# First shift and scale in four batches, k-outer projections, and a later place for the slabs that VectorE weighs

## What is computed

```python
mod = jax.nn.silu(c) @ w_ada[l] + b_ada[l]
shift1, scale1, gate1, shift2, scale2, gate2 = jnp.split(mod[:, None, :], 6, axis=-1)
h = rms_norm(x, g_norm1[l]) * (1.0 + scale1) + shift1
proj = h @ w_in[l]
na_q, na_k, na_v, q_lat, kv_lat, k_rot, gate_na, gate_mla = jnp.split(proj, split_at, axis=-1)
qa = rms_norm(na_q.reshape(B, S, NA_HEADS, NA_HEAD_DIM), g_na_q[l])
ka = rms_norm(na_k.reshape(B, S, NA_HEADS, NA_HEAD_DIM), g_na_k[l])
```

## Time and profile before

| | us |
|---|---|
| three runs | 1152.79, 1153.98, 1155.91 |
| median | 1153.98 |
| the profiled execution's own time | 1156.07 |
| its span | 1154.20 |
| TensorE matmul busy | 1102.4 (96%) |
| VectorE busy | 408.7 (35%) |
| ScalarE busy | 298.5 (26%) |
| mean granted TensorE clock | 0.982 of full |

### The profile page before, as it was taken

One profiled execution on the slowest core, in us unless ns is written; L12 is line 12 of the kernel. 1 busy time (PEld: TensorE's weight loads), 2 busy tenths in 40 slices (PEclk: granted clock), 3 DMA queues, 4 the chain that ended last, 5 costly groups with the idle time before them and its releaser, 6 DMA issues.

```text
span 1154.2 us, 18227 instructions
## 1 busy us (share of the span) xinstructions
PE 1102.4 (96%) x7154; PEld 740.6 (64%) x7154; DVE 408.7 (35%) x993; ACT 298.5 (26%) x635; POOL 53.4 (5%) x85
## 2 busy tenths in 40 slices
PE   5899999999999899998899999999899999999998
PEld 2787686688756445544555455554368888887567
DVE  0599765532724121221212122212134111341951
ACT  1214324601511121221211112112123121212951
POOL 0010202003000000000000000000001001100001
PEclk8899899999999999998999999999999999999999
DMA  9999447944699999999999999999994334230000
GB/s 384 384 403 411 164 146 299 420 194 183 263 367 412 408 410 377 410 410 364 410 380 410 397 410 409 395 410 409 411 372 145 111 114 157 79 125 1 1 1 37
DMA packets 75495, 334.51 MB, mean 290 GB/s; under 512 B 8432, under 2 KB 9808, under 8 KB 59792
## 3 DMA queue, kind: packets, MB, share of 16 engines
q1 hardware_dynamic: 73008, 327.97, 72.2%
q10 hardware_dynamic: 2176, 3.37, 0.8%
q0 software_dynamic: 224, 1.97, 0.4%
HBM read 332.23 MB, written 1.05 MB: 289 GB/s over the span
## 4 chain that ended last, share of the span: by engine, by line
PE 83%; DMA 10%; DVE 4%; SPq 1%; issue 1%; ACT 1%; ACTq 0%; DVEq 0%
PE bank L930 13%; PE bank L490 11%; PE bank L974 7%; DMA ring<-experts 7%; PE bank L812 5%; PE bank L832 5%; PE bank L1065 5%; PE bank L886 4%; PE bank L1166 2%; PE bank L505 2%; PE bank L722 2%; PE bank L1117 2%; PE bank L737 2%; PE bank L397 2%; DMA ring<-stream 2%; PE bank L556 2%
## 5 line engine op out<-in xcount | busy, mean ns | idle before, releaser
L930 PE MATMUL bank<-ring,arena 128*32 128x512 f32 (+1 forms) x1120 | 182.0, 626 | 16.9 <-DMA ring<-experts 16.7
L490 PE MATMUL bank<-hT,ring 128*128 128x256 f32 x704 | 156.9, 384 | 1.7 <-ACT hT L1359 1.7
L490 PEld LDWEIGHTS bank<-hT,ring 128*128 128x128 f32 x704 | 134.9, 193 | 23.1 <-issue 4.6
L930 PEld LDWEIGHTS bank<-ring,arena 128*32 128x32 f32 (+1 forms) x1120 | 52.3, 124 | 127.7 <-issue 127.4
L974 PE MATMUL bank<-ring,arena 128*32 128x512 f32 (+1 forms) x560 | 87.5, 596 | 2.0 <-DMA ring<-experts 2.0
L812 PE MATMUL bank<-arena 128*128 128x128 bf16 x1152 | 72.2, 219 | 1.1 <-ACT arena L1516 1.1
L812 PEld LDWEIGHTS bank<-arena 128*128 128x128 bf16 x1152 | 66.9, 98 | 8.0 <-issue 5.0
L832 PE MATMUL bank<-arena 128*128 128x512 bf16 x288 | 66.1, 379 | 0.0
L2122 DVE TENSOR_TENSOR arena<-bank,arena 128x512 f32<-128x512 f32 x48 | 33.2, 692 | 92.3 <-ACT arena L1542 92.3
L2110 DVE SCALAR_TENSOR_TENSOR arena<-bank,arena 128x256 f32<-128x256 f32 x24 | 11.6, 484 | 145.2 <-ACT arena L1535 141.3
L1293 POOL TENSOR_TENSOR hT<-hT 128x256 f32<-128x256 f32 x30 | 21.8, 726 | 859.1 <-ACT hT L1353 857.7
(11 more groups left out here) (369 smaller groups left out, 1435.7 us busy)
## 6 DMA issues: line engine op xcount, KB each, us to landing
ring<-experts SPq DMA_DIRECT2D x384, 512.0 KB, 11.3
ring<-stream SPq DMA_DIRECT2D x118, 1024.0 KB, 9.3
arena<-consts POOLq DMA_DIRECT2D x1, 1664.0 KB, 11.7
resid<-x SPq DMA_DIRECT2D x1, 1024.0 KB, 5.3
resid<-ctx ACTq DMA_DIRECT2D x1, 1024.0 KB, 12.5
arena<-stream SPq DMA_DIRECT2D x1, 1024.0 KB, 9.3
arena<-rpb ACTq DMA_DIRECT2D x2, 438.0 KB, 25.7
out<-arena SPq DMA_DIRECT2D x3, 256.0 KB, 2.3
```

The source lines that it names most:

```text
L490: mm = mmul(o[:, 0:n_tok], w[:, k, t * P:(t + 1) * P], hT[:, k, 0:n_tok], start=(k == 0), stop=(k == KT - 1))
L930: mm = mmul(o[at:at + n_slots, :], xg[:, kk, at:at + n_slots], w[g][:, k, :], start=(kk == 0), stop=(kk == KT - 1))
```

## The change

ada1 0 to 7 become four batches ("first", i) of two slabs, i and i+4, so that each gives the shift and the scale of k = 2i and 2i+1; each batch has its own copy, fold, bias, gain, two scales and two shifts. The projections qk0 and qk1 run k-outer: after each batch, both tiles of a slab advance by two k (two_ks: four matmuls), each of their four tiles in a bank of its own (0 to 3); part of qk2 runs between (banks 4 and 5). The slab order begins ada1 0, 4, in0, ada1 1, 5, in1, ada1 2, 6, 3, 7, in2, in3. The sums over the heads' squares of all eight tiles move behind the tiles of qk3 and vna0, in banks 6 and 7. ScalarE issues its three loads of constants behind the fourth copy. The weighed slabs stand later in the stream: eight up to in7, then one each behind in7, gate stage 0, ukv and gate stage 1. VectorE weighs 0 to 7 before the latents' means, 8 and 9 behind the latents, 10 and 11 ahead of the drains of msum. TensorE adds the sums in gate stages 1, 2, 3, 5 and 6.

```diff
--- before.py
+++ after.py
@@ -338,13 +338,21 @@

         GATE_FILL = [[("ada1", 8)], [], [("ada1", 21)], [("ada1", 22)], [], [], [], [("ada1", 23)]]
         SIDE = list(range(9, 21))
+        SIDE_SUMS = {1: range(0, 4), 2: range(4, 6), 3: range(6, 8), 5: range(8, 10), 6: range(10, 12)}
         side_slabs = []
-        ADA_BATCHES = [("ada1", 0, 8), ("ada1", 8, 16), ("ada2", 0, 12), ("ada2", 12, 12)]
+        ADA_BATCHES = {1: ("ada1", 8, 16), 2: ("ada2", 0, 12), 3: ("ada2", 12, 12)}
+        FIRST_BATCHES = [("first", i) for i in range(4)]

         def ada_batch(which, j):
-            for n, (w, lo, count) in enumerate(ADA_BATCHES):
+
+            if which == "ada1" and j < 8:
+                return ("first", j % 4), j // 4
+            for n, (w, lo, count) in ADA_BATCHES.items():
                 if w == which and lo <= j < lo + count:
                     return n, j - lo
+
+        def batch_size(batch):
+            return 2 if batch in FIRST_BATCHES else ADA_BATCHES[batch][2]

         EARLY = [("na", i) for i in range(4)] + [("mla", i) for i in range(4)]
         FIRST_FILL = [("ada2", j) for j in range(4)]
@@ -387,7 +395,7 @@
                 w, n = take_slab((which, j))
                 w = w.rearrange("p (k c) -> p k c", k=8)
                 batch, r = ada_batch(which, j)
-                first, last = r == 0, r == ADA_BATCHES[batch][2] - 1
+                first, last = r == 0, r == batch_size(batch) - 1
                 if first:
                     open_group((batch, "quarters"), 6)
                 o = bk((batch, "quarters"))
@@ -606,26 +614,82 @@
             pe.wait_ge(S("ones_set"), 1)
             rms_sums("sum1", 0, 256, squared="sq1")
             pe.wait_ge(S("silu_c"), 1)
-            for j in range(8):
-                ada_slab("ada1", j)
+
+            in_at = {}
+
+            def first_inputs(slab, t, ks):
+
+                name = (f"qk{slab}", t)
+                if slab not in in_at:
+                    in_at[slab] = take_slab(("in", slab))[1]
+                o = open_group(name, 2 * slab + t) if ks[0] == 0 else bk(name)
+                for k in ks:
+                    h_tile("h1", k)
+                    mm = mmul(o[:, 0:256], eight(in_at[slab])[:, k, t * P:(t + 1) * P], hT[:, k, 0:256], start=(k == 0), stop=(k == KT - 1))
+                if ks[-1] == KT - 1:
+                    close_group(mm, name)
+                    if t == 1:
+                        slab_end[in_at[slab]] = name
+
+            def head_squares(j):
+                pe.wait_ge(S("sq_qk"), j + 1)
+                o = open_group(("qkn", j), 6 + j % 2)
+                close_group(mmul(o[:, 0:256], cc("bones"), sqt[:, j % 2, 0:256], start=True, stop=True), ("qkn", j))
+
+            def two_ks(slab, i):
+                for t in range(2):
+                    first_inputs(slab, t, (2 * i, 2 * i + 1))
+
+            ada_slab("ada1", 0)
+            ada_slab("ada1", 4)
             pe.wait_ge(S("fold_in"), 16)
-            ada_fold(0)
-
-            for s in range(4):
-                t_tiles(f"qk{s}", ("in", s), 2, [1, 2], 256, ready="h1" if s == 0 else None)
-                for i in ((0,), (1,), (2, 3), (4, 5))[s]:
-                    leave_to_vector(i)
-                for t in range(2):
-                    j = 2 * s + t
-                    pe.wait_ge(S("sq_qk"), j + 1)
-                    o = open_group(("qkn", j), 3 + j % 2)
-                    close_group(mmul(o[:, 0:256], cc("bones"), sqt[:, j % 2, 0:256], start=True, stop=True), ("qkn", j))
-            for s in range(2):
-                tok_tiles(f"vna{s}", ("in", 4 + s), 2, [1, 2])
-                for i in ((6, 7), (8, 9))[s]:
-                    leave_to_vector(i)
+            ada_fold(("first", 0))
+            two_ks(0, 0)
+            ada_slab("ada1", 1)
+            ada_slab("ada1", 5)
+            ada_fold(("first", 1))
+            two_ks(1, 0)
+            two_ks(0, 1)
+            two_ks(1, 1)
+            ada_slab("ada1", 2)
+            ada_slab("ada1", 6)
+            ada_fold(("first", 2))
+            ada_slab("ada1", 3)
+            two_ks(0, 2)
+            ada_slab("ada1", 7)
+            two_ks(1, 2)
+            ada_fold(("first", 3))
+            first_inputs(2, 0, range(0, 6))
+            two_ks(0, 3)
+            two_ks(1, 3)
+            first_inputs(2, 0, range(6, KT))
+            first_inputs(2, 1, range(KT))
+
+            w, n = take_slab(("in", 3))
+            w = w.rearrange("p (k c) -> p k c", k=8)
+            for i in (0, 1):
+                leave_to_vector(i)
+            for t in range(2):
+                o = open_group(("qk3", t), t)
+                for k in range(KT):
+                    mm = mmul(o[:, 0:256], w[:, k, t * P:(t + 1) * P], hT[:, k, 0:256], start=(k == 0), stop=(k == KT - 1))
+                close_group(mm, ("qk3", t))
+                head_squares(2 * t)
+                head_squares(2 * t + 1)
+            slab_end[n] = ("qk3", 1)
+            _, n = take_slab(("in", 4))
+            for i in (2, 3):
+                leave_to_vector(i)
+            for t in range(2):
+                tok_tile(("vna0", t), n, t, 2 + t)
+                head_squares(4 + 2 * t)
+                head_squares(5 + 2 * t)
+            slab_end[n] = ("vna0", 1)
+            tok_tiles("vna1", ("in", 5), 2, [1, 2])
+            for i in (4, 5):
+                leave_to_vector(i)
             t_tiles("ql", ("in", 6), 2, [1, 2], 256)
-            for i in (10, 11):
+            for i in (6, 7):
                 leave_to_vector(i)
             w, n = take_slab(("in", 7))
             w = w.rearrange("p (k c) -> p k c", k=8)
@@ -640,6 +704,7 @@
                               start=(kk == 0), stop=(kk == 1))
             close_group(mm, "krot4")
             slab_end[n] = "krot4"
+            leave_to_vector(8)
             pe.wait_ge(S("sq_ql"), 2)
             rms_sums("sum_ql", 5, 256, tiles=2, src=lambda k: sqt[:, k, 0:256])
             pe.wait_ge(S("sq_kvl"), 1)
@@ -652,12 +717,12 @@
                 t_tiles(f"gt{s}", ("in", 8 + s), 2, [1, 2], 256)
                 for f in GATE_FILL[s]:
                     ada_slab(*f)
-                if s < 2:
-                    for i in range(6 * s, 6 * s + 6):
-                        side_sum(i)
+                for i in SIDE_SUMS.get(s, ()):
+                    side_sum(i)

             pe.wait_ge(S("small_set"), 4)
             gate_tiles(0)
+            leave_to_vector(9)

             pe.wait_ge(S("qln"), 2)
             w, n = take_slab(("uq", 0))
@@ -682,7 +747,9 @@
                 o = open_group(("uv", t), 1 + t % 2)
                 close_group(mmul(o[:, :], lat[:, 2, t * P:(t + 1) * P], w[:, 512:1024], start=True, stop=True), ("uv", t))
             slab_end[n] = ("uv", 1)
+            leave_to_vector(10)
             gate_tiles(1)
+            leave_to_vector(11)

             gate_tiles(2)
             o = open_group("mq_sums", 3)
@@ -1334,8 +1401,9 @@
             def ada_quarters(batch):

                 full(act, (batch, "quarters"))
-                if batch:
-                    full(act, (batch - 1, "columns"))
+                before = dict(zip(FIRST_BATCHES[1:] + [1, 2, 3], FIRST_BATCHES + [1, 2])).get(batch)
+                if before:
+                    full(act, (before, "columns"))
                 emptied(a.copy(quarters[:], bk((batch, "quarters"))[:, 0:256]), (batch, "quarters"))

             def root(n, src, tag, cols, parts=P):
@@ -1344,10 +1412,6 @@
                 a.activation(src[0:parts, 0:cols], src[0:parts, 0:cols], ACT.Sqrt).then_inc(S(tag + "_rt"), 1)

             root(1, rstd, "n1", 256)
-            ada_quarters(0)
-            act.dma_start(cs[:, C_EARLY:C_W], consts_d[:, C_EARLY:C_W]).then_inc(S("const_in"), 16)
-            act.dma_start(stat[0:96, 0:256].bitcast(I32), pos_d).then_inc(S("const_in"), 16)
-            act.dma_start(ve[:, V_EARLY:V_W], vecs_d[:, V_EARLY:V_W]).then_inc(S("const_in"), 16)
             def square(tag, k, side=0):

                 a.activation(hT[:, k, T * side:T * side + T], xT[:, side, k, :], ACT.Square).then_inc(S(tag), 1)
@@ -1363,8 +1427,14 @@
                 a.activation(mark2[0:1, 0:1], ones[0:1, 0:1], f)


-            for k in range(KT):
-                shift("h1", k, mod1[:, k:k + 1])
+            for i in range(4):
+                ada_quarters(("first", i))
+                if i == 3:
+                    act.dma_start(cs[:, C_EARLY:C_W], consts_d[:, C_EARLY:C_W]).then_inc(S("const_in"), 16)
+                    act.dma_start(stat[0:96, 0:256].bitcast(I32), pos_d).then_inc(S("const_in"), 16)
+                    act.dma_start(ve[:, V_EARLY:V_W], vecs_d[:, V_EARLY:V_W]).then_inc(S("const_in"), 16)
+                for k in (2 * i, 2 * i + 1):
+                    shift("h1", k, mod1[:, k:k + 1])
             for r in range(2):
                 src = bass.AP(rpb_d.tensor, (5 - r) * 31 - 48, [[1, 64], [15 * 31, 8], [1, RUN]])
```

(36 more changed lines are left out.)

## The result

The changed kernel takes 1161.57 us in the median of five runs (1159.87 to 1163.94) against 1153.98 for the kernel before. The ratio, estimated from all runs, is 1.0054, with a 95% interval of 1.0028 to 1.0081: a small loss, but clear of no change. In a second batch it was 1160.40 against 1155.49, ratio 1.0060 (1.0039 to 1.0081). The forecast was 1152.6 with a range of 1148 to 1159: the sign is wrong and the median lies outside. The profiled execution took 1159.87 us with a span of 1158.1; before's had 1154.20.

What follows compares the result with a forecast made beforehand. VectorE's chain was taken as the new bound. Gate stage 3 2.55 us earlier, side sums +0.28 and an early clock spell +0.9 gave -1.4 from the median 1153.98: 1152.6 us, range 1148.0 to 1159.0.

Steps and rivals of the forecast that it cites:

- The hole in the loads: in3 waits for qk0 to close at 41.6; stream loses 8 us, taken as nothing; as rival up to 3 us, 14%.
- Front, TensorE: TensorE's start through qk3: first projection piece at 17.0, end at 47.7 us, from full-clock prices.
- clock spell at the front, 0.9: TensorE's idle from 14.2 to 17.0 may drop the clock for one piece: 0 to 1.7 us, 0.9 taken.
- loses 1: TensorE, ready at 59.8, waits for the bank of head squares 4 and 5, emptied at 60.6.
- 10.4 us like for like: Front's gain by the end of the third projected slab: 59.8-1.7-47.7.
- From the latent mean to the first shuffle 22.67: VectorE's old stretch, carried over; slabs 8 and 9 add 7.82, putting the shuffle at 116.3 us.
- The third sum at the end of weighing plus 0.4: Third sum of squares waits for slabs 10 and 11, weighed by 137.6, and starts at 138.0 us.
- Clock behind the wait, 2.6: Low clock after the wait for the drains, before gate stage 3: between 0 and 3.4 us, 2.6 taken.
- 36.90 plus 0.28 for four side sums: Gate stage 3 to the scores: 36.90 us as before, plus 0.28 for four side sums now there.
- The hole costing nothing: Rival, 17%: before the third sum of squares, clock holds or recovers (1150.0), or drains are not held (1143.4).
- The early clock staying low until 34 us: Slower rival, 17%: low clock from near 17 us shifts VectorE's chain by 6.5, total 1158.2 us.
- the 21% for slower: Whole kernel: chance of a time above 1157.5 us, 0.15 of it from the early clock staying low.

Runs made afterwards that it cites:

- late2: The changed kernel with the weighing of slabs 10 and 11 put behind VectorE's four drains of the sums of squares: 1156.72 us, ratio 1.0020.
- late4: The changed kernel with slabs 8 to 11 weighed behind the four drains, their places in the stream moved to match: 1150.71 us, ratio 0.9957.
- warm_hole: The changed kernel with five idle matmuls in TensorE's wait between second and third sum of squares: 1162.15 us, ratio 1.0039.
- sqrt_early: The changed kernel with ScalarE's table for roots loaded right behind the sines: 1161.13 us, ratio 1.0043.
- mix: late4 with side sums in two lots, gate stage 3 between one-column groups two and three, key square sums in banks 0 and 5: 1156.09 us, ratio 0.9994.
- mix2: As mix, but gate stage 3 in banks 0 and 5 and the sums of squares in 1 and 2 again: 1152.08 us, ratio 0.9972.

## Why the prediction was wrong

**The way the change works was right in its main steps.** The hole in the loads (no bytes at 36 to 38 us), TensorE's wait ahead of the one-column sums (3.12, "some 2.5" forecast), the wait for the drains between second and third sum (3.73, "some 5"), and the low clock behind it all came at the places named. late2 and late4 show that the weighing of slabs 8 to 11 makes both waits. The rule from the Trainium skill (TensorE: Matmul & The Clock Gate, Part 1), that activity releases the throttle, agrees with the traces behind this wait: low in the changed kernel, full behind the idle matmuls of warm_hole. It does not tell where the clock fell: that was within 131 to 132, ahead of the wait, under one-column matmuls with a busy share of 1.00.

**The sum was wrong, because it stood 1.4 us from zero and its errors all had one sign.** Forecast scores were 181.78-1.4, 180.4; the trace has 186.07, 5.7 later. By the prediction's own steps:

- "Front, TensorE", with "clock spell at the front, 0.9": the latent mean was forecast at 85.8, 86.7 with the spell, and came at 88.55, +1.85. The first ada slabs started 0.56 late (12.90 instead of 12.34), as the sums of squares of x had taken 6.01 instead of 5.49. The spell cost 1.5, not 0.9: the first piece started 0.7 behind the forecast (17.70), the three pieces behind the second fold 2.2 behind (24.13 against 21.9), and in late2 and late4, which have no early spell, nothing is lost between these two points. qk3 waited 0.38 for its slab, whose load took 6.4 us instead of 4.7 and was put at nothing. The other 0.3 is small change, most of it between qk3's first tile and the first weighed slab. Adding up back-to-back work was not at fault: late2 is 1.1 behind at the first piece and 0.8 behind at the end of the last one, and VectorE's stretch from the first weighed slab to the latent mean, 33.4 forecast, took 33.43. The 0.99 of wait was forecast, as "loses 1". The "10.4 us like for like" is 8.3 by the same arithmetic (59.8-1.7-49.78).
- "From the latent mean to the first shuffle 22.67": +1.68. I carried a distance over from the old trace in which ScalarE's table load had been hidden, as VectorE was late there. Once VectorE was early, ScalarE's 1.28 us load stood on the path. sqrt_early shows 1.26 of it; the other 0.3 of wait is TensorE's last matmuls for the rotated key, which ScalarE copies ahead of the root (to 89.89).
- "The third sum at the end of weighing plus 0.4": +0.49. The drain took 0.8, not 0.4, after a weighed slab.
- "Clock behind the wait, 2.6": measured (3.49-1.72)+(7.89-7.07), 2.59. The size is right; that it is right to 0.01 is luck, as it was picked between 0 and 3.4 from one spell of 2.5 elsewhere.
- "36.90 plus 0.28 for four side sums": +1.66. Six sums in three lots, not four in two, lie there. A lot of two costs 0.53 to 0.56; the 0.28 allows 0.07 a sum and names no row, and before, six sums had taken 0.96.

These are 1.85+1.68+0.49+1.66, 5.68. **The steps that failed are three terms of the sum.** The front was taken 1.85 too early, with its clock spell too short and its wait for a slab at nothing. The stretch from the latent mean to the shuffle, 22.67, was taken as fixed, though an engine that used to arrive late now arrived first: it was 24.4 (120.73-88.55, less 7.82 of weighing). The side sums were put at 0.28 and cost 1.9, of which 1.65 are their own three lots.

The median lies 9.0 us above the forecast, and the scores are 5.7 of that. The forecast took its difference from one traced execution, 2.09 above its median, and the changed kernel's trace is of one 1.70 below its median: that is 3.8, and the stretch behind the scores gives 0.4 back.

**The rivals.** The hole costing nothing (17%): excluded by late2, where removing it moves gate stage 3 by 4.7 us against the one-column sums. The early clock staying low until 34 us: it did fall, and returned after 3 us. The hole in the loads: 0.38 us at qk3 in the first trace, 0.29 to 0.79 in the others with this front; in the first trace no weighing waited for its slab. The measured result lies on the side of the slower rival, but not by its mechanism; the 21% for slower was too little for a forecast whose chain was VectorE's, with TensorE ahead of it: there every missed microsecond of VectorE counts in full.

**What stays open.** The traces show 3.6 to 4.3 us at the scores; the two ratios have their middles at 6 to 7 us. One interval includes 4, the other begins at 4.5. The same gap stands in every run: set against before, the time (by its ratio) lies 1 to 5 us further to the slow side than the scores do. late2 is the plainest, with scores 2.4 us earlier than before and a time of 1.0020. Part of it can be that before's only trace is of an execution 2.09 us above its median; the clock spell of 1.6 right behind the scores, in five of the eleven traces other than before's, is another part in those runs. The stretch behind the scores varies by more than 5 us from trace to trace, and the rest was not settled.

## What to carry to other kernels

When one engine is made earlier, find which engine holds it next and go through that engine's program in order: work that filled an idle stretch before is on the path afterwards. Move such filler behind the last thing others wait for; here four slabs moved by a few lines turned a loss of some 6 us into a gain of 5. And re-derive each distance between two events from what each waits for, since a distance measured while one partner was late hides the other's cost.

## What the runs showed that I had not expected

A matmul of 32 columns of weights that adds one side sum costs about 0.5 us whether one lot holds two or four (0.53 to 0.56, and 0.57), and 1.00 for eight. The granted clock fell while TensorE ran one-column matmuls without a pause: in the earlier trace rows at 136 to 137 with a busy share of 1.00, and in late4 within 128 to 129. With a gate stage between their two halves, in mix and mix2, it did not fall there, and the eight records of 512 columns took 3.94 and 3.93 us instead of 7.05. Two traces are few for a clock whose low stretches also move by a few us from one execution to the next, so this is what the rows show and not a rule.
